# Two small reorderings in a fused two-block layer kernel: the mixer's front, and the tail of the recurrence

## What is computed

```python
(q_n, k_c, v_c, k_s, v_s, k_w, v_w, g_nsa, q_f, k_f, v_f, f_logit,
 gate_a, gate_b) = split_cols(h @ w_in, IN_SPLITS)
...
# compressed keys and values: 15 overlapping blocks of 32 tokens, per group
flat = blocks.transpose(0, 1, 3, 2, 4).reshape(b, nc, g, CMP_BLOCK * d)
return jax.nn.gelu(flat @ w1) @ w2
...
# forgetting attention: cumulated log-sigmoid of the forget logits, as a bias
c = jnp.cumsum(jax.nn.log_sigmoid(f_logit), axis=1)
sc = jnp.einsum('bhqd,bkhd->bhqk', qi, k) + ci[..., None] - c[:, :, None, :]
...
y = jax.nn.sigmoid(gate_a) * (o_nsa @ w_up_nsa) + jax.nn.sigmoid(gate_b) * (o_fox @ w_up_fox)
return y @ w_out
```

```python
# second block, after the state recurrence y = wkv7(...)
mean = jnp.mean(y, axis=-1, keepdims=True)
var = jnp.mean(jnp.square(y - mean), axis=-1, keepdims=True)
y = (y - mean) * lax.rsqrt(var + GN_EPS) * gn_g + gn_b
y = y + jnp.sum(rh * kh * r_k, axis=-1, keepdims=True) * vh
out = (y.reshape(B, T, C) * g) @ wo
```

## Time and profile before

| | |
|---|---|
| median of 3 runs | 1523.21 us (1520.97 to 1532.89) |
| the profiled execution | 1531.64 us, of which its span 1530.2 us |
| TensorE matmul busy | 1423.7 us, 93% of the span |
| VectorE busy | 952.5 us, 62% |
| ScalarE busy | 713.3 us, 47% |
| DMA | 221.43 MB, mean 145 GB/s |
| mean granted TensorE clock | 0.952 of full |

### The profile page before, as it was taken

One profiled execution on the slowest core, in us unless ns is written; L12 is line 12 of the kernel. 1 busy time (PEld: TensorE's weight loads), 2 busy tenths in 40 slices (PEclk: granted clock), 3 DMA queues, 4 the chain that ended last, 5 costly groups with the idle time before them and its releaser, 6 DMA issues. The chain is left out here.

```text
span 1530.2 us, 28913 instructions
## 1 busy us (share of the span) xinstructions
PE 1423.7 (93%) x12764; PEld 1364.3 (89%) x12764; DVE 952.5 (62%) x1307; ACT 713.3 (47%) x1096; POOL 7.1 (0%) x12
## 2 busy tenths in 40 slices
PE   7999999997799999999979987988999996889999
PEld 7999998796699899999979986778999984789999
DVE  4655575357775446666579864556666688466665
ACT  5444454145554445444438513335444464354443
POOL 0000000000000000000000010000000000000000
PEclk9999999988999999999989986999999997999999
DMA  6554545341144334555514400013555530244552
GB/s 255 211 198 169 191 161 183 139 182 56 71 181 163 111 138 159 200 193 189 197 55 169 166 2 30 29 38 128 197 189 188 199 138 1 111 148 184 194 192 84
DMA packets 32949, 221.43 MB, mean 145 GB/s; under 512 B 3855, under 2 KB 5263, under 8 KB 6584
## 3 DMA queue, kind: packets, MB, share of 16 engines
q1 hardware_dynamic: 31768, 218.51, 39.5%
q10 hardware_dynamic: 1056, 1.07, 0.2%
HBM read 218.49 MB, written 1.06 MB: 143 GB/s over the span
## 5 line engine op out<-in xcount | busy, mean ns | idle before, releaser
L302 DVE TENSOR_TENSOR tile_lo<-ring,tile_hi 128x1024 fp32r<-128x1024 f32 x396 | 476.4, 1223 | 341.5 <-ACT tile_hi L292 340.4
L292 ACT ACTIVATE tile_hi<-ring 128x1024 fp32r<-128x1024 f32 x396 | 408.2, 1054 | 303.2 <-PE ps L344 292.8
L342 PE MATMUL ps<-hT_hi,tile_hi 128*128 128x256 f32 x1664 | 476.9, 287 | 16.8 <-DVE hidden_lo L751 7.6
L343 PE MATMUL ps<-hT_lo,tile_hi 128*128 128x256 f32 x1664 | 472.8, 284 | 0.0
L344 PE MATMUL ps<-hT_hi,tile_lo 128*128 128x256 f32 x1664 | 472.7, 284 | 0.0
L342 PEld LDWEIGHTS ps<-hT_hi,tile_hi 128*128 128x128 f32 x1664 | 320.6, 193 | 23.7 <-issue 9.4
L343 PEld LDWEIGHTS ps<-hT_lo,tile_hi 128*128 128x128 f32 x1664 | 320.5, 193 | 0.0
L344 PEld LDWEIGHTS ps<-hT_hi,tile_lo 128*128 128x128 f32 x1664 | 320.2, 192 | 0.0
L342 PE MATMUL ps<-hidden_hi,tile_hi 128*128 128x256 f32 x864 | 239.5, 277 | 0.0
L343 PE MATMUL ps<-hidden_lo,tile_hi 128*128 128x256 f32 x864 | 239.5, 277 | 0.0
L344 PE MATMUL ps<-hidden_hi,tile_lo 128*128 128x256 f32 x864 | 239.4, 277 | 0.0
(11 more groups left out here) (461 smaller groups left out, 2137.5 us busy)
## 6 DMA issues: line engine op xcount, KB each, us to landing
ring<-stream SPq DMA_DIRECT2D x204, 1024.0 KB, 4.8
x_sb<-x SPq DMA_DIRECT2D x4, 256.0 KB, 4.0
bias<-f_dram ACTq DMA_DIRECT2D x1, 1024.0 KB, 7.3
squares<-mem SPq DMA_DIRECT2D x1, 1024.0 KB, 4.7
out<-x_sb SPq DMA_DIRECT2D x4, 256.0 KB, 2.2
const_sb<-const SPq DMA_DIRECT2D x1, 577.0 KB, 9.3
small_sb<-small SPq DMA_DIRECT2D x1, 493.5 KB, 9.5
cum<-g_tail SPq DMA_DIRECT2D x1, 128.0 KB
```

The lines of the kernel that those rows point to most:

```text
L292: act.activation(e.w_hi[:, n % SPLIT, :], e.ring[:, tile % RING, span(n % 2, HALF)], ACT.Copy).then_inc(e.tile_hi.handle, 1)
L302: dve.tensor_tensor(e.w_lo[:, n % SPLIT, :], e.ring[:, CUT[n // 2] % RING, span(n % 2, HALF)], e.w_hi[:, n % SPLIT, :].bitcast(F32), ALU.s ...
L342: pe.matmul(out, left[0], right[0], start=start, stop=False)
L343: pe.matmul(out, left[0], right[1], start=False, stop=False)
```

## The change

In the mixer's front:

- The stream's order changes. The four RAW tiles are now two and two, with a gate tile (`gate_next`) between them.
- The eight forget spreads no longer stand ahead of the `gate_first` tile but inside it, one after every second set of three products.
- The gate tiles go to banks 7, 7, 5, 7. The transposes of the compressed hidden rows stand in the middle of the third gate tile, between its two halves. The compressed scores go to banks 6 and 1.
- VectorE copies the bias row and the logits ahead of the rests of the same step, and not behind them.

In the recurrence's tail: `centre(0)`, `sums(0)`, `spreads(0)` and `spreads(1)` stand one step earlier on TensorE, `variance(0)`, `inverse(0)`, `centre` and the square root one or two steps earlier on the other engines; the spreads of quarter 1 use another bank and no longer wait for the first norm; `spreads(2)` and `spreads(3)` stand in the middle of `half_tile(1, 0)`; VectorE does `variance(1)`, `norm(2)` and `norm(3)` ahead of the rests of the weight tiles that stood before them.

No instruction is added to or taken from the arithmetic.

```diff
-    ("ffn1", 3 * D_FF // 256), ("mix", 11), ("gate_first", 1), ("cmp", 4), ("gates", 7), ("up", 4), ("mixout", 4),
+    ("ffn1", 3 * D_FF // 256), ("mix", 11), ("gate_first", 1), ("cmp0", 2), ("gate_next", 1), ("cmp1", 2),
+    ("gates", 6), ("up", 4), ("mixout", 4),
...
+    gate_bank = (7, 7, 5, 7)
+    pc_banks = (6, 1)
...
-            pe.wait_ge(*mirrored.at(1))
-            pe.wait_ge(*summed.at(1))
-            for h in range(HEADS):
...
-            mm.then_inc(*forgets_done.one())
...
-            filler(0)
-            for half in range(2):
...
-            filler(1)
-            filler(2)
-            pe.wait_ge(*fox_bias_built.at(1))
...
+            pe.wait_ge(*mirrored.at(1))
+            for mt in range(2):
+                wt = chunks_of(arrived(e, pe, gf, mt))
+                for k in range(KC):
+                    mm = product(pe, e.ps[:, gate_bank[0], span(mt, SEQ)], cut(wt, ALL, k, ALL), cut(e.hT, ALL, k, ALL),
+                                 k == 0, k == KC - 1)
+                    if k == 0 and mt == 0:
+                        pe.wait_ge(*summed.at(1))
+                    if k % 2 == 0:
+                        spreading = spread_forget(4 * mt + k // 2)
+                mm.then_inc(*e.tile_done.one())
+            spreading.then_inc(*forgets_done.one())
...
+            hidden_products(0)
+            pe.wait_ge(*filled.at(1))
+            col_to_T(e, pe, gates_from[1], e.hT, gate_bank[1])
+            hidden_products(1)
             pe.wait_ge(*fox_bias_built.at(1))
+            col_to_T(e, pe, gates_from[2], e.hT, gate_bank[2], between=turn_hidden)
...
             copy_filler(0)
             heads_after(e, act, 2 * (gf + 1))
-            tile_after(e, act, g0 + 3)
+            copy_filler(1)
+            heads_after(e, act, 2 * (gates_from[1] + 1))
+            tile_after(e, act, raw_tiles[1] + 1)
             for kind in range(2):
...
-            copy_filler(1)
             copy_filler(2)
...
-                rests_before(e, dve, g + n + 1)
...
                 if n == 3:
                     bias.vector(dve, 7)
                 if n == 4:
                     dve.wait_ge(*gates_done.at(1))
                     dve.tensor_tensor(logits[:, :], e.ps[0:32, 7, 0:SEQ], e.scale[0:32, :], ALU.mult).then_inc(*logits_copied.one())
+                rests_before(e, dve, g + n + 1)
```

```diff
-    centre_bank, spread_bank = (7, 7, 0, 1), (7, 7, 3, 0)
+    centre_bank, spread_bank = (7, 7, 0, 1), (7, 3, 3, 0)
...
                 if h == 1:
-                    pe.wait_ge(*normed.at(1))
+                    pe.wait_ge(*gram_kept.at(16))
+                elif h == 2:
+                    pe.wait_ge(*normed.at(2))
+                elif h == 3:
+                    pe.wait_ge(*centred.at(3))
...
-                if n in (10, 11):
-                    centre(n - 10)
-                if n == 13:
+                if n in (9, 11):
+                    centre((n - 9) // 2)
+                if n == 12:
                     sums(0)
-                if n in (16, 17):
-                    spreads(n - 16)
+                if n in (15, 16):
+                    spreads(n - 15)
...
-            half_tile(1, 0)
-            spreads(2)
-            pe.wait_ge(*centred.at(3))
-            spreads(3)
+            half_tile(1, 0, between=lambda: (spreads(2), spreads(3)))
...
-                if n in (11, 12):
-                    centre(n - 11)
-                if n == 15:
+                if n in (10, 11):
+                    centre(n - 10)
+                if n == 13:
                     square_root(0)
...
+            variance(1)
             rests_after(e, dve, 2 * g0 + 1)
-            variance(1)
             inverse(1)
-            rests_after(e, dve, 2 * g0 + 3)
             norm(2)
             norm(3)
             rests(2)
+            rests_after(e, dve, 2 * g0 + 3)
             rests(3)
```

More of the change, by code:

```diff
@@ L76 @@
 TILES = _at
-RAW = [FIRST[name] + n for name, count in (("cmp", 4), ("lora_a", 1), ("lora_g", 1)) for n in range(count)]
+RAW = [FIRST[name] + n for name, count in (("cmp0", 2), ("cmp1", 2), ("lora_a", 1), ("lora_g", 1)) for n in range(count)]
 CUT = [g for g in range(TILES) if g not in RAW]
@@ L1274, in _, with turn_hidden @@
                 mm.then_inc(*e.tile_done.one(4))
-            filler(1)
-            filler(2)
-            pe.wait_ge(*fox_bias_built.at(1))
[L1278 to L1282, removed]
-            tr.then_inc(*hidden_turned.one())
+            def turn_hidden():
+                for kind in range(2):
+                    pe.wait_ge(*gelu_done.at(kind + 1))
+                    for mt in range(2):
+                        tr = pe.transpose(e.ps[:, 2 - 2 * kind, 32 * mt:32 * mt + NB], hidden_rows[rows_of(kind), span(mt, P)],
+                                          const(e, "ident")[rows_of(kind), rows_of(kind)])
+                tr.then_inc(*hidden_turned.one())
+            pe.wait_ge(*mirrored.at(1))
+            for mt in range(2):
+                wt = chunks_of(arrived(e, pe, gf, mt))
[8 more added lines that the diff above has]
+            spreading.then_inc(*forgets_done.one())
+            pe.wait_ge(*blocks_ready.at(2))
+            pe.wait_ge(*evacuated[1].at(7))
+            pe.wait_ge(*evacuated[0].at(2))
+            hidden_products(0)
+            pe.wait_ge(*filled.at(1))
+            col_to_T(e, pe, gates_from[1], e.hT, gate_bank[1])
+            hidden_products(1)
+            pe.wait_ge(*fox_bias_built.at(1))
+            col_to_T(e, pe, gates_from[2], e.hT, gate_bank[2], between=turn_hidden)
             pe.wait_ge(*hidden_copied.at(1))
@@ L1443, in _ @@
             rests_after(e, dve, 2 * (gf + 1))
-            for n in range(FILLERS - 1):
-                rests_before(e, dve, g0 + 5 + n)
+            rests_after(e, dve, 2 * (gates_from[1] + 1))
+            rests_before(e, dve, gates_from[2] + 1)
             dve.wait_ge(*hidden_turned.at(1))
@@ L2810, in _, with half_tile @@
             mark_tail(e)
-            def half_tile(i, k):
+            def half_tile(i, k, between=None):
                 if k == 0:
@@ L2816, in half_tile @@
                 for m in range(KC):
+                    if between and m == KC // 2:
+                        between()
                     mm = product(pe, e.ps[:, 4 + m // 2, span(m % 2, SEQ)], cut(wt, ALL, span(m, P)),
@@ L2888, in _ @@
             square_root(1)
+            heads_after(e, act, 2 * g0 + 2)
+            heads(2)
             heads_after(e, act, 2 * g0 + 3)
-            heads(2)
             heads(3)
@@ L2951, in _ @@
                                                  in1=w.first_scale[:, :], op0=ALU.mult, op1=ALU.mult)
+                if n == 13:
+                    variance(0)
                 if n == 14:
[L2953 to L2954 removed]
                     inverse(0)
@@ L3281, in lay_out_stream @@
             cols(w[half * D:(half + 1) * D])
-    tiles.extend(gates[1:])
+        tiles.extend(gates[1 + half:2 + half])
+    tiles.extend(gates[3:])
     cols(np.concatenate([i["w_up_nsa"][0][paired(HEADS)], i["w_up_fox"][0]]))
```

55 lines of the change are left out of this document (26 added, 29 removed).

## The result

The changed kernel takes 1514.67 us (median of 14 runs, 1509.45 to 1523.12) against 1529.82 us of the kernel before beside it (14 runs, 1520.97 to 1534.09): ratio 0.9918, 95% interval 0.9898 to 0.9939. That is a gain of 12.5 us (9.3 to 15.6), where 20.0 were forecast (the two medians alone are 15.2 apart; gains are read from the ratios here). As a time 1503 us was forecast, and the range ended at 1512. The profiled execution took 1510.41 us, its span 1509.1 us at a mean clock of 0.955 (before 0.952).

The account below looks back on a forecast made before the run. TensorE, busy 93% of the span, bounds the kernel by its work, idle time and granted clock. Terms 5.1 + 6.9 + 8.0 = 20.0 us take the profiled 1531.64 to 1511.6, scaled from median 1523.2 to 1503 us; range 1496 to 1512.

Parts of the forecast that it names:

- The copies ahead of the rests: Mixer's front: waits for logits (2.8 us) and bias row (0.6) go, and 1.7 of low clock; 5.1 us.
- The tail: Recurrence's tail: waits for centred quarter, spreads and last quarters shrink or go, with low clock behind; 8.0 us.
- The front: Mixer's front, spreads and gate tile between compressed weights: 3.4 + (3.7 - 0.5) + 1.7 + 0.7 - 2.1 = 6.9 us.
- The spreads inside the gate tile: Mixer's front: spreads cost the same between dense products, and low clock from 285 to 292 us goes; 3.4 us.
- The rival of the exposed weight loads: Spreads inside the gate tile: weight loads don't overlap, 16 x 0.185 = 3.0 us lost, 1506 us; chance 10%.
- Idle time: After the RAW products in the front: a gate tile fills TensorE's idle time, 0.5 us of 3.7 stay.
- the bank: Mixer's front: the bank change removes TensorE's 0.7 us wait for a gate copy.
- The Gelu: Third gate tile: TensorE waits about 2.1 us at the transposes for ScalarE's Gelu, behind the fourth gate tile's heads.
- The clock behind the idle time: Mixer's front, behind the 3.7 us idle time: the low clock there goes too; 1.7 us.
- the first rival's second half: The wait for the Gelu with tiny transposes behind it opens a new low-clock stretch, 1.7 us; whole rival's chance 15%.
- loads that share the DMA engines: Front: three loads served together, RAW tile lands at 9.9, TensorE idles 4.1 and drops its clock; 1509 us; chance 5%.
- The slower case: Front from 282 us to the end of the scores all at 1.2 GHz, costing 28 us: 1531 us; chance 2%.

Follow-up runs that it names:

- A: The kernel before with only VectorE's copies of bias row and logits moved ahead of the rests: 1523.73 us against 1528.54, ratio 0.9966.
- C: The kernel before with only the recurrence's tail changed: 1521.26 us, ratio 0.9948.
- B: The kernel before with only the front's new order, from the spreads to the Gelu: 1527.54 us, ratio 1.0004.
- the early Gelu: Changed kernel, ScalarE's gate copy and Gelu ahead of the fourth gate tile's heads, VectorE's following rests behind the compressed-values copy: 1508.89 us, ratio 0.9883; again 1512.64, 0.986.
- the table's second row: B alone and three profiles of the change, last mirrored product to first transposed weights: 55.6, 57.0, 58.5, 58.5 us, mean 57.4.
- A and C: The changed kernel with its front as before, so copies and tail only: 1515.64 us against 1530.08 of the kernel before, ratio 0.9903.

## Why the prediction was wrong

**Level.** The forecast was scaled to the median of three runs, 1523.2 us. The kernel before took 1527.1 to 1530.4 in the medians of 11 to 31 runs beside each later kernel, and its profiled execution, 1531.64, was nearer to these. This alone is 4 to 7 us: from 1529 the same 20 us lead to 1509, inside the range. The level is not why the gain fell short: 12.5 us were measured beside the kernel before. The range's allowance for "a median that three runs leave open by some us" was made on the low side only.

**The copies ahead of the rests: right.** Forecast 5.1, measured 5.2 (0.9 to 9.6), so that the two agree to 0.1 is luck. The stretch from the bias product to the first mirrored one is firmer: 38.1 or 38.2 us in all eleven profiles of kernels with A, 41.9 to 44.7 in the five without. The waits for logits and bias row are gone, and so is the low clock behind them; it stands in four of the five without A.

**The tail: right.** Forecast 8.0, measured 8.0 (4.4 to 11.6); here too the equal figures are luck, the steps are not. The wait for the last quarters is 0.5 us (0.4 forecast), and the low clock behind it, 3.4 to 6.8 us in all five profiles without C, stands in none of the eleven with it. Norms 2 and 3 of the change, VectorE's timeline:

```profile
1003.34 0.69 DVE L2935 TENSOR_TENSOR before<-before,ps 128x512 f32<-128x512 f32 x1 [2.12 <-PE ps L2806]
...
1006.83 0.69 DVE L2937 TENSOR_TENSOR before<-before,cum 128x512 f32<-128x512 f32 x1
1007.44 0.68 DVE L2941 TENSOR_TENSOR hT_lo<-before,hT_hi 128x512 fp32r<-128x512 f32 x1
```

The first half tile began at about 993.5, so they stand 9.8 to 14.6 us behind it, within a microsecond of the forecast's 9.0 to 14.0.

**The front: wrong, 6.9 forecast, -0.6 and 1.2 measured in the time, 2.0 in the stretch.** Its terms one by one:
- *The spreads inside the gate tile, +3.4.* This is the step that failed. It took the 6.8 us at 0.57 of the earlier trace rows as what a block of thin products costs. The same kernel's second profile has 1.00 there; over six profiles with the block the low clock costs 1.3 us on average. "Nothing gained and nothing lost" for the spreads' own time was the other half of the error: between products they cost 2.7 us more. Together -1.4 in place of +3.4, so 4.8 us, which is all that the stretch is short of (6.9 - 2.0 = 4.9). The evidence for the clock holding, 1.00 from 986 to 1011 us, was of the same kind: the second profile has 6.8 us at 1.2 GHz in that stage, from 996 to 1004.
- *The rival of the exposed weight loads* had 3.0 us for this, 16 records at 0.185; measured is 2.7, 0.17 a record. Its size is right. That the loads are the cause fits the rows above, where load and product start together at both ends of a spread, but no run separated the loads from what else a switch costs. The Trainium skill, TensorE: Matmul & The Clock Gate, "Part 3: Packing small matmuls", has loads overlap products only when their row groups differ; by that rule no load at either end of a spread overlaps, since spreads and products share a row group. The trace agrees there, and does not between dense products, which share theirs too: their loads start 0.11 us ahead.
- *Idle time, +3.2, and the bank, +0.7.* Right: 3.7 to 4.0 became 0.2 to 0.4, and 0.7 went, in every profile with B.
- *The Gelu, -2.1.* It is -2.5, by the chain of steps that was given (which in its own figures, 14.6 less 12.7, makes 1.9). The table load took 1.28 us with 0.02 or less on either side of it (301.84 + 1.05, 302.90, 304.20), so the 2.7 us that the prediction set against the row are not in this chain.
- *The clock behind the idle time, +1.7.* Near in size, but not by the step that was given. The wait for the Gelu has its own low stretch of 3.4 us behind it in five of six profiles (none in B alone), which is the first rival's second half, so the low clock behind the idle time was traded for another. Against that the low clock of 322 to 330, left out of the sum, stands in all five profiles without B and in three of those six. From the first product of the compressed weights to the first transposed weights the kernels without B took 36.6 us on average and those in the table's second row 33.2, 3.4 less. Of these about 2.1 are waits, which leaves 1.3 for the clock. With the early Gelu the clock is 1.00 there in four profiles of five, and the same piece takes 28.2 us.

So the front's sum is -1.4 for the spreads and 3.4 for all the rest, where 3.4 and 3.5 were forecast.

Of the other rivals, loads that share the DMA engines did not show: no RAW tile was waited for. The slower case did not come near.

## What to carry to other kernels

A low-clock stretch that one profile shows beside thin work is a sample, not a price: look at a second execution of the same kernel before its clock is counted as a gain; one behind an idle gap of TensorE (2.4 to 4.0 us here) came back in nearly every profile, and in nearly every one went when the gap did. A thin product put between dense ones cost 0.34 us more each time than in a block, while the block lost 1.3 us to the clock on average: price both, from more than one profile, before choosing. When a wait is removed by reordering, follow what else the next engine's queue holds: here the Gelu stood behind a head that had to wait for a load, and moving it ahead took 5.0 us from the stretch, where the whole reordering of the front took 2.0. In the time it is some 4 us, of which the noise leaves only the sign likely.

## What the runs showed that was not expected

- Unchanged stages of the code differ by several microseconds between executions: from the start to the bias product 219.3 to 224.3 us, with no low clock in the first 200 us; the attention stage 50.5 to 52.6 us, with 17 to 27 us at 1.2 GHz. Each is as large as a term of the forecast.
- Idle time of TensorE adds up where clock does not, to within what two profiles of one kernel differ by. Its waits sum to 103.1 and 101.6 us in the two profiles of the kernel before, 97.8 with A, 98.0 with B, 95.5 with C, 90.2 with A and C, and 85.9, 89.0 and 89.8 in three profiles of all three. The parts give 18.0 less than the first of these figures; all three give 13.3 to 17.2 less. TensorE's busy time can't be compared at this size: it is 1423.7 and 1420.2 us in the two profiles of the kernel before.
